# Expert weights laid out as 128 neighbouring rows per k tile, in a one-core encoder layer with a mixture of experts

## The chip, the cores and the metric

The kernel runs on one core of a Trainium2 chip. The metric is device time in microseconds, lower is better. A core has a matrix engine (PE, its weight loads are shown apart as PEld), a vector engine (DVE), a scalar engine (ACT), a general one (POOL), and a synchronising engine (SP) whose instruction stream issues here every DMA. The DMAs of the core are spread over 16 DMA engines.

## The reference

One layer of an encoder for 256 frames of width 2048, all float32. With everything but the last part in one line each:

```python
xn = rms_norm(h, norm_mix_g); proj = xn @ w_in + b_in             # attention and gating branches
merged = g_a * (y_a @ w_branch_a) + g_b * (y_b @ w_branch_b)
h = h + merged @ w_out
xn2 = rms_norm(h, norm_ffn_g)
# hierarchical mixture of experts: top-1 of 4 groups, top-2 of its 8 experts, 32 experts of width 256
hid = silu(t @ w_e_gate[e]) * (t @ w_e_up[e])                     # w_e_gate, w_e_up: (32, 2048, 256)
out = out + (hid * combine[:, e]) @ w_e_down[e]                   # w_e_down: (32, 256, 2048)
return rms_norm(h + out, norm_final_g)
```

The three expert weights are 201 MB of the 310 MB that the kernel moves.

## The kernel before

**Dense part.** All projections but the experts' run as "pieces" of a weight matrix. SP loads a piece of 1 MB (four k tiles of 128 rows by 512 columns) in two DMAs into one of four buffers `raw`; a weight row contributes 2 KB. ACT makes a rounded high part `whi` (line 529), DVE the rest `wlo` (line 831), and PE multiplies both with high and low parts of the activations (lines 1303 to 1305). The last four rounds are `w_out`; between them SP issues the first loads of expert weights.

**Router.** After the last dense round come the router and its top-k (from line 1511 on PE and line 1128 on DVE). A few matmuls whose result is not used (line 1310) fill PE's waits.

**Experts.** The 32 experts are taken in 8 quads of 4. An expert has room for 32 tokens, so a quad fills 128 columns. For each quad:

- `gather(qd)` (line 1602): for each of 16 k tiles PE multiplies the residual rows, as stationary operand, by the selection matrix `sel` of the quad. That picks the quad's tokens and turns them, two matmuls (two halves of the tokens) to a k tile. ACT (line 727) and DVE (line 1184) take the result out of PSUM into `xe`, times the gain of the norm for the 128 model columns of that k tile.
- `gate_up(qd, j, k4)` (line 1551): expert j against four k tiles of gate and up weights in one slot; the partial sums of four column groups are added by `fold_parts` (line 1568).
- `down`, `scatter`, and the addition into the residual (lines 1583, 1654, 1225).

`gather(qd + 1)` stands between the third and the fourth expert of quad qd; `gather(0)` stands alone, ahead of everything.

**Order of the loads.** The expert weights go through a ring of 18 slots of 1 MB. `load_slot(n)` fills one: a gate/up slot by two DMAs of 512 KB (line 435), a down slot by one DMA of 1 MB (line 428; line 431 for the last quad). A quad is 24 slots, 16 of gate and up and 8 of down; in all 192 slots. Slots 0 to 17 are loaded while the dense part runs, in pairs between the `w_out` rounds and then as dense buffers come free. From slot 18 on SP waits until PE has used slot n - 18, and issues in order.

**Which model rows a k tile holds.** With `"e (p k) f -> e p k f"` partition p holds rows 16p to 16p + 15, and k tile k is every sixteenth row. The four k tiles of a slot are then four neighbouring rows of 256 floats: one run of 4 KB in memory for each partition. The gather has to follow the same order, so it reads every sixteenth column of `resid`:

```python
rows = resid[:, t, :].rearrange("p (d k) -> p k d", k=KT)[:, 4 * q + h, :]
```

and the gain has to be loaded in that order too, as `gP` (line 417). The gains in the other order (column kt holds the gains of rows 128 kt to 128 kt + 127) lie already in `gT`, made at the kernel's start. The down weights are loaded in runs of 8 KB, for the last quad in runs of 2 KB.

A fallback (`If(more == 1)`) for experts with more than 32 tokens is not entered with these inputs.

Of the kernel before, what the change touches and what calls it, by code (L numbers as in the profile page):

```python
# [28 lines left out]
ALU = mybir.AluOpType  # L29
ACT = mybir.ActivationFunctionType  # L30
AX_X = mybir.AxisListType.X

P = 128
# [31 lines left out]
def build_trunk(nc, a, out):  # L65
    T, D = a["x"].shape[1], a["x"].shape[2]
    TT, KT = T // P, D // P
# [25 lines left out]
    with ExitStack() as ctx:  # L93
# [4 lines left out]
        def at(name, kb, shape, dt=F32):  # L98
            nbytes = 4
            for n in shape[1:]:  # L100
                nbytes *= n
            assert kb * KB + nbytes <= room, name
            return nc.alloc_sbuf_tensor_at(name, shape, dt, offset=base + int(kb * KB))

        def sem(name):
            return ctx.enter_context(nc.semaphore(name))
# [4 lines left out]
        resid = at("resid", 0, [P, TT, D])  # L111
# [56 lines left out]
        qT = at("qT", 197.5, [HEAD, T // CHUNK, Q_PER_KV, CHUNK])  # L168
        kT = at("kT", 201.5, [HEAD, T])
        prob = [at(f"prob{b}", 202.5 + 2 * b, [P, 4, P]) for b in range(2)]  # L170
        gP = at("gP", 199, [P, KT])
        wr = at("wr", 194.5, [P, KT, NR])
        small_at = [206.5]

# [11 lines left out]
        gT = small("gT", [P, 2 * KT])  # L186
# [61 lines left out]
        resid_in, g2_in, wr_in, br_in, gf_in = (sem(n) for n in ("resid_in", "g2_in", "wr_in", "br_in", "gf_in"))  # L248
# [35 lines left out]
        xe_full, xe_by_act, xe_by_dve = sem("xe_full"), sem("xe_by_act"), sem("xe_by_dve")  # L284
# [4 lines left out]
        f_in, f_xT_full, f_xT_made, f_gu_full = sem("f_in"), sem("f_xT_full"), sem("f_xT_made"), sem("f_gu_full")  # L289
# [60 lines left out]
        w_a_v, w_b_v = chunked(a["w_branch_a"]), chunked(a["w_branch_b"])  # L350
        b_in_v = a["b_in"].rearrange("a (c n) -> a c n", n=COLS)
        b_gate_v = a["b_gate"].rearrange("a (c n) -> a c n", n=COLS)
        wg_v = a["w_e_gate"][0].rearrange("e (p k) f -> e p k f", p=P)
        wu_v = a["w_e_up"][0].rearrange("e (p k) f -> e p k f", p=P)
        wd_v = a["w_e_down"][0].rearrange("e (k p) d -> e p k d", p=P)

        def wide(row):
# [5 lines left out]
        def _(sp):  # L363
# [50 lines left out]
            for t in range(TT):  # L414
                sp.dma_start(resid[:, t, :], x_v[:, t, :]).then_inc(resid_in, 16)
            sp.wait_ge(yaT_lo_made, NKV)
            sp.dma_start(gP[:], a["norm_ffn_g"].rearrange("a (p k) -> (a p) k", k=KT)).then_inc(g2_in, 16)
            sp.dma_start(wr[:, :, 0:NG], a["w_router_group"][0].rearrange("(k p) n -> p k n", p=P)).then_inc(wr_in, 16)
            sp.dma_start(wr[:, :, LG:NR], a["w_router_expert"][0].rearrange("(k p) n -> p k n", p=P)).then_inc(wr_in, 16)
            def load_slot(n):  # L420
# [70 lines left out]
            for u in range(2 * TT):  # L491
                t, h = divmod(u, 2)
# [30 lines left out]
        def _(act):  # L523
# [21 lines left out]
            for u in range(8):  # L545
# [3 lines left out]
                t, k4 = divmod(u, 4)  # L549
# [172 lines left out]
            def gathered_a(qd, q):  # L722

                act.wait_ge(xe_full, KT // 4 * qd + q + 1)
                for h in range(4):
                    kt = 4 * q + h
                    act.activation(xe[:, qd % 2, kt, :, :].rearrange("p e s -> p (e s)"),
                                   bank[6 + q % 2][:, h * P:(h + 1) * P], ACT.Copy,
                                   scale=gP[:, kt:kt + 1]).then_inc(xe_by_act, 1)

            def gate_up_out(qd, j):

# [57 lines left out]
            with act.If(more == 1):  # L790
                act.activation(table_junk[:, 0:1], ones[:, 0:1], ACT.Silu).then_inc(f_table, 1)
                act.wait_ge(f_table, 1)
                for t in range(TT):
                    for k4 in range(4):
                        act.wait_ge(f_xT_full, 4 * t + k4 + 1)
                        for k in range(4):
                            kt = 4 * k4 + k
                            act.activation(xT_f[:, kt, :], bank[6 + k4 % 2][:, k * P:(k + 1) * P],
                                           ACT.Copy, scale=gP[:, kt:kt + 1]).then_inc(f_xT_made, 1)
                    with act.Fori(0, NE) as e:  # L800
                        act.wait_ge(f_gu_full, e + (NE * t + 1))
                        act.activation(f_s[:], bank[0][:, 0:FF], ACT.Silu,
                                       scale=rstd[:, 2 * TT + t:2 * TT + t + 1]).then_inc(f_silu_made, 1)
                        act.wait_ge(f_hT_full, e + (NE * t + 1))
                        act.activation(f_hT[:], bank[1][:, 0:2 * P].rearrange("p (a b) -> p a b", a=2),
                                       ACT.Copy).then_inc(f_hT_made, 1)
                act.wait_ge(f_added, 4 * NE * TT + 4)
                act.wait_ge(sq_f_made, TT * NC)
                for b in range(NC):
                    final_squares(b, f_sq_made)  # L810
                act.wait_ge(f_hf, TT * NC)
                act.activation(table_junk[:, 0:1], ones[:, 0:1], ACT.Sqrt).then_inc(table_back, 1)
                act.wait_ge(table_back, 1)
            root(3)
            for t in range(TT):
                n = 3 * TT + t
                if t == 0:
# [3 lines left out]
                               scale=rstd[:, n:n + 1]).then_inc(y_by_act, 1)  # L821
# [3 lines left out]
        def _(dve):  # L825
# [75 lines left out]
            for h2 in range(2):  # L901
                rows = slice(h2 * CHUNK, (h2 + 1) * CHUNK)
# [199 lines left out]
            evac_out(0)  # L1102
            for k in range(1, ROUND):
                dense_lo(D_ROUND0 + 1, k)
            dve.wait_ge(g2_in, 16)
            with dve.Fori(2, NC) as n:
                dense_lo(n + D_ROUND0, 0)
                evac_out(n - 1)
# [73 lines left out]
            def gathered_v(qd, q):  # L1182
                dve.wait_ge(xe_full, KT // 4 * qd + q + 1)
                dve.tensor_tensor(xe[:, qd % 2, 4 * q:4 * q + 4, :, :].rearrange("p k e s -> p k (e s)"),  # L1184
                                  bank[6 + q % 2][:].rearrange("p (k n) -> p k n", k=4),
                                  gP[:, 4 * q:4 * q + 4].to_broadcast([P, 4, P]), ALU.mult).then_inc(xe_by_dve, 1)

            pick(0)
            gathered_v(0, 1)
# [69 lines left out]
            with dve.If(more == 1):  # L1259
# [9 lines left out]
                for t in range(TT):  # L1269
                    with dve.Fori(0, NE) as e:  # L1270
# [6 lines left out]
                        for b in range(NC):  # L1277
                            h = resid[:, t, b * COLS:(b + 1) * COLS]
# [22 lines left out]
        def _(pe):  # L1301
# [300 lines left out]
            def gather(qd):  # L1602

                pe.wait_ge(sel_made, qd + 1)
                for q in range(KT // 4):
                    if q == 0 and qd:
                        pe.wait_ge(selT_made, qd)
                        pe.wait_ge(added, 8 * (qd - 1))
                    if q == 2:
                        pe.wait_ge(xe_by_act, 8 * qd + 4)  # L1610
                    if q == 3:
                        pe.wait_ge(xe_by_dve, 2 * qd + 1)
                    for h in range(4):
                        for t in range(TT):
                            rows = resid[:, t, :].rearrange("p (d k) -> p k d", k=KT)[:, 4 * q + h, :]
                            mm = pe.matmul(bank[6 + q % 2][:, h * P:(h + 1) * P], rows,  # L1616
                                           sel[:, t, :, :].rearrange("p e s -> p (e s)"), start=t == 0, stop=t == TT - 1)
                    mm.then_inc(xe_full, 1)
# [77 lines left out]
            with pe.If(more == 1):  # L1696
                pe.wait_ge(added, 8 * NQ)
                for t in range(TT):
                    if t:
                        pe.wait_ge(f_added, 4 * NE * t + 4)  # L1700
                    for k4 in range(4):
                        if k4 > 1:
                            pe.wait_ge(f_xT_made, 16 * t + 4 * k4 - 4)
                        for k in range(4):
                            dst = bank[6 + k4 % 2][:, k * P:(k + 1) * P]
                            rows = resid[:, t, :].rearrange("p (d k) -> p k d", k=KT)[:, 4 * k4 + k, :]
                            mm = pe.matmul(dst, rows, ident[:], start=True, stop=True)
                        mm.then_inc(f_xT_full, 1)
                    pe.wait_ge(f_xT_made, 16 * t + 16)
                    with pe.Fori(0, NE) as e:  # L1710
                        pe.wait_ge(f_in, 48 * e + (48 * NE * t + 48))
                        pe.wait_ge(f_added, 4 * e + (4 * NE * t + 4))
                        for kt in range(KT):
                            mm = pe.matmul(bank[0][:], xT_f[:, kt, :], f_gu[:, :, kt, :], start=(kt == 0), stop=(kt == KT - 1))
                        mm.then_inc(f_gu_full, 1)
                        pe.wait_ge(f_hid_made, e + (NE * t + 1))
                        for f in range(2):
                            mm = pe.transpose(bank[1][:, f * P:(f + 1) * P], f_hid[:, f * P:(f + 1) * P], ident[:])
                        mm.then_inc(f_hT_full, 1)
                        pe.wait_ge(f_hT_made, e + (NE * t + 1))  # L1720
                        for f in range(2):
                            for b in range(NC):
                                mm = pe.matmul(bank[2 + b][:], f_hT[:, f, :], f_dn[:, f, b * COLS:(b + 1) * COLS],
                                               start=(f == 0), stop=(f == 1))
                        mm.then_inc(f_dn_full, 1)
# [22 lines left out]
```

## Time and profile before

| | |
|---|---|
| time, median of 3 runs | 1064.36 us (1061.12 to 1065.03) |
| the profiled execution: its own time | 1064.98 us |
| its span | 1063.3 us |
| PE busy | 977.3 us (92%) |
| PE weight loads busy | 687.6 us (65%) |
| DVE, ACT busy | 392.5 us (37%), 335.2 us (32%) |
| moved by DMA | 310.17 MB, mean 292 GB/s |
| mean granted PE clock | 0.971 |

The span runs from the first to the last instruction; the 1.7 us between it and the execution's time lie around it. "Busy" of PE counts overlapping matmuls as one stretch. The granted clock is given as a share of 2.4 GHz, so 0.50 is 1.2 GHz. Shares over the whole span mix the dense part (to about 578 us) with the experts (from there on).

### The profile page before, as it was taken

The numbers are of one execution on the slowest core, as the hardware profiler recorded it, in microseconds if no ns is written. First come the engines' busy times: TensorE is split into PE (matmuls) and PEld (weight loads), VectorE is DVE, ScalarE is ACT, GpSimd is POOL, SyncE is SP. The second block draws the span as 40 slices with busy tenths as digits, with TensorE's granted clock in tenths as the row PEclk, the third lists the DMA queues.
The fourth block names the chain that finished last, engine by engine and source line by source line (L and its number), as shares of the span: only waits on it lengthen the run. The fifth ranks groups of instructions, "written<-read, shape, count | busy, mean of one in ns | idle before, by whom it ended". The sixth has DMA issues, their size and how long they took to land.

```text
span 1063.3 us, 13009 instructions
## 1 busy us (share of the span) xinstructions
PE 977.3 (92%) x5154; PEld 687.6 (65%) x5154; DVE 392.5 (37%) x530; ACT 335.2 (32%) x485; POOL 2.7 (0%) x13
## 2 busy tenths in 40 slices
PE   6999999999999999999999899998888878788884
PEld 5888888788888888888888564554362625335221
DVE  5545556565455455565343102020202011020204
ACT  5335545654343333444443111111011111101123
POOL 1000000000000000000000000000000000000000
PEclk9999999999999999999999999999998999899968
DMA  9565444458666656767777599999999999999994
GB/s 318 198 207 171 165 162 158 163 172 263 222 198 198 203 191 216 246 210 255 256 261 277 215 393 415 413 411 416 409 418 409 416 412 412 416 409 418 409 396 172
DMA packets 108820, 310.17 MB, mean 292 GB/s; under 512 B 13241, under 2 KB 14305, under 8 KB 101345
## 3 DMA queue, kind: packets, MB, share of 16 engines
q1 hardware_dynamic: 108770, 309.46, 77.8%
q8 instruction: 36, 0.59, 0.2%
q14 instruction: 14, 0.11, 0.0%
HBM read 307.33 MB, written 2.10 MB: 291 GB/s over the span
## 4 chain that ended last, share of the span: by engine, by line
PE 68%; DMA 19%; SPq 7%; ACT 3%; DVE 2%; issue 1%; ACTq 0%; DVEq 0%
PE bank L1303 15%; PE bank L1305 15%; PE bank L1304 15%; DMA slot<-in_w_e_up 11%; DMA slot<-in_w_e_down 7%; PE bank L1564 6%; SPq L435 5%; PE bank L1616 4%; PE bank L1583 4%; PE bank L1654 2%; SPq L428 2%; PE bank L1572 1%; PE bank L1407 1%; PE bank L1431 1%; ACT whi L529 1%
## 5 line engine op out<-in xcount | busy, mean ns | idle before, releaser
L831 DVE TENSOR_TENSOR wlo<-raw,whi 128x2048 fp32r<-128x2048 f32 x92 | 210.7, 2291 | 211.3 <-ACT whi L529 211.3
L529 ACT ACTIVATE whi<-raw 128x2048 fp32r<-128x2048 f32 x92 | 176.2, 1916 | 257.6 <-PE bank L1305 257.6
L1303 PE MATMUL bank<-whi,actT_hi 128*128 128x512 f32 x608 | 240.0, 395 | 3.9 <-DVE actT_lo L862 2.2
L1305 PE MATMUL bank<-wlo,actT_hi 128*128 128x512 f32 x608 | 236.9, 390 | 0.0
L1304 PE MATMUL bank<-whi,actT_lo 128*128 128x512 f32 x608 | 236.8, 389 | 0.0
L1564 PE MATMUL bank<-slot,xe 128*32 128x512 f32 x1024 | 125.7, 618 | 24.2 <-DMA slot<-in_w_e_up 22.3
L1303 PEld LDWEIGHTS bank<-whi,actT_hi 128*128 128x128 f32 x608 | 114.2, 188 | 30.1 <-DVE wlo L831 2.8
L1305 PEld LDWEIGHTS bank<-wlo,actT_hi 128*128 128x128 f32 x608 | 114.2, 188 | 24.1
L1304 PEld LDWEIGHTS bank<-whi,actT_lo 128*128 128x128 f32 x608 | 114.2, 188 | 22.7
L1616 PEld LDWEIGHTS bank<-sel,resid 128*128 128x128 f32 x512 | 112.4, 311 | 6.9 <-issue 6.4
L1616 PE MATMUL bank<-sel,resid 128*128 128x128 f32 x512 | 113.9, 385 | 0.0
L1225 DVE TENSOR_TENSOR resid<-bank,resid 128x512 f32<-128x512 f32 x64 | 44.3, 691 | 149.7 <-PE bank L1654 149.6
L1583 PE MATMUL bank<-slot,hid 128*32 128x512 f32 x512 | 69.4, 690 | 26.0 <-DMA slot<-in_w_e_down 21.4
L1564 PEld LDWEIGHTS bank<-slot,xe 128*32 128x32 f32 x1024 | 30.0, 112 | 97.4 <-issue 73.7
L1654 PE MATMUL bank<-out_rows,selT 128*128 128x512 f32 x128 | 62.8, 613 | 3.5 <-ACT out_rows L746 1.7
L1583 PEld LDWEIGHTS bank<-slot,hid 128*32 128x32 f32 x512 | 18.1, 123 | 69.5 <-issue 64.0
L734 ACT ACTIVATE gu_rows<-bank 128x512 f32<-128x512 f32 x32 | 19.1, 597 | 139.1 <-PE bank L1564 139.1
L1184 DVE TENSOR_TENSOR xe<-bank,gP 128x512 f32<-128x512 f32 x16 | 11.1, 691 | 134.6 <-PE bank L1616 134.6
L1572 PEld LDWEIGHTS bank<-fold,gu_rows 128*128 128x128 f32 x256 | 32.5, 196 | 31.3 <-ACT gu_rows L734 26.5
L1654 PEld LDWEIGHTS bank<-out_rows,selT 128*128 128x128 f32 x128 | 20.0, 188 | 47.6 <-issue 47.6
L1217 DVE TENSOR_TENSOR hid<-bank,s_act 128x64 f32<-128x64 f32 x32 | 7.2, 225 | 107.9 <-ACT s_act L738 107.9
L746 ACT ACTIVATE out_rows<-bank 128x512 f32<-128x512 f32 x32 | 19.1, 597 | 83.0 <-PE bank L1583 83.0
(198 smaller groups left out, 670.2 us busy)
## 6 DMA issues: line engine op xcount, KB each, us to landing
slot<-in_w_e_gate SPq DMA_DIRECT2D x128, 512.0 KB, 14.6
slot<-in_w_e_up SPq DMA_DIRECT2D x128, 512.0 KB, 15.3
slot<-in_w_e_down SPq DMA_DIRECT2D x64, 1024.0 KB, 19.1
raw<-in_w_gate SPq DMA_DIRECT2D x64, 512.0 KB, 4.6
raw<-in_w_in SPq DMA_DIRECT2D x56, 512.0 KB, 4.8
raw<-in_w_out SPq DMA_DIRECT2D x32, 512.0 KB, 4.8
raw<-in_w_branch_a SPq DMA_DIRECT2D x16, 512.0 KB, 4.6
raw<-in_w_branch_b SPq DMA_DIRECT2D x16, 512.0 KB, 4.3
```

Source lines behind the costliest of these rows:

```text
L435: sp.dma_start(dst[:, h * KB:(h + 1) * KB].rearrange("p (k f) -> p k f", f=FF), w[QUAD * qd + j, :, 4 * k4:4 * k4 + 4, :]).then_inc(slot_i ...
L529: return act.activation(whi[slot][:], src, ACT.Copy)
L831: dve.tensor_tensor(wlo[s][:], raw[:, k, :], whi[s][:], ALU.subtract).then_inc(lo_made, 1)
L1225: dve.tensor_tensor(h, bank[dst][:], h, ALU.add).then_inc(added, 1)
L1303: pe.matmul(o, x_hi, w_hi, start=start, stop=False)
L1304: pe.matmul(o, x_lo, w_hi, start=False, stop=False)
L1305: return pe.matmul(o, x_hi, w_lo, start=False, stop=stop)
L1564: mm = pe.matmul(bank[j % 2][c * CAP:(c + 1) * CAP, :], xe[:, qd % 2, 4 * k4 + c, j, :], w[:, :, c, :], start=k4 == 0, stop=k4 == 3)
L1572: mm = pe.matmul(bank[j % 2][:, f * CAP:(f + 1) * CAP], gu_rows[j % 2][:, f * P:(f + 1) * P], fold[:], start=True, stop=True)
L1583: mm = pe.matmul(bank[2 + b][e * CAP:(e + 1) * CAP, :], hid[:, e, f * CAP:(f + 1) * CAP], w, start=f == 0, stop=f == 1)
L1616: mm = pe.matmul(bank[6 + q % 2][:, h * P:(h + 1) * P], rows, sel[:, t, :, :].rearrange("p e s -> p (e s)"), start=t == 0, stop=t == TT - 1)
L1654: pe.matmul(bank[dst][:], selT[:, t * P:(t + 1) * P], out_rows[:, b * COLS:(b + 1) * COLS], start=True, stop=True).then_inc(scat_full, 1)
```

## The change

The gate and up weights are read so that k tile k is the 128 neighbouring rows 128k to 128k + 127. A partition's part of a slot is then four runs of 1 KB, 128 rows apart in memory, where it was one run of 4 KB. The bytes, the slots, the tiles in SBUF and the matmuls are the same in number and size. The gather reads 128 neighbouring columns of `resid` in place of every sixteenth. The gain comes from the second half of `gT`, and `gP`, its DMA and DVE's wait for it are gone. The down weights are loaded as before.

```diff
-        gP = at("gP", 199, [P, KT])
...
-        wg_v = a["w_e_gate"][0].rearrange("e (p k) f -> e p k f", p=P)
-        wu_v = a["w_e_up"][0].rearrange("e (p k) f -> e p k f", p=P)
+        wg_v = a["w_e_gate"][0].rearrange("e (k p) f -> e p k f", p=P)
+        wu_v = a["w_e_up"][0].rearrange("e (k p) f -> e p k f", p=P)
...
-            sp.dma_start(gP[:], a["norm_ffn_g"].rearrange("a (p k) -> (a p) k", k=KT)).then_inc(g2_in, 16)
...
-                                   scale=gP[:, kt:kt + 1]).then_inc(xe_by_act, 1)
+                                   scale=gT[:, KT + kt:KT + kt + 1]).then_inc(xe_by_act, 1)
...
-            dve.wait_ge(g2_in, 16)
...
-                                  gP[:, 4 * q:4 * q + 4].to_broadcast([P, 4, P]), ALU.mult).then_inc(xe_by_dve, 1)
+                                  gT[:, KT + 4 * q:KT + 4 * q + 4].to_broadcast([P, 4, P]), ALU.mult).then_inc(xe_by_dve, 1)
...
-                            rows = resid[:, t, :].rearrange("p (d k) -> p k d", k=KT)[:, 4 * q + h, :]
+                            rows = resid[:, t, (4 * q + h) * P:(4 * q + h + 1) * P]
```

The fallback's reads of `resid` and of the gain change in the same way.

## Rows read from the trace of the kernel before

**Rows 1.** The page: DMA share and GB/s in 40 slices

```profile
span 1063.3 us, 13009 instructions
...
DMA  9565444458666656767777599999999999999994
GB/s 318 198 207 171 165 162 158 163 172 263 222 198 198 203 191 216 246 210 255 256 261 277 215 393 415 413 411 416 409 418 409 416 412 412 416 409 418 409 396 172
```

**Rows 2.** Windows (length, busy and count by engine, granted clock, DMA share, GB/s), whole stages

```profile
440.00:540.00 100.00, 100.00 (x483) 83.83 (x482) 52.72 (x41) 42.04 (x38) 0.00 (x0) 1.00 0.69 242
...
705.00:1015.00 310.00, 256.06 (x1571) 134.51 (x1571) 44.73 (x86) 42.07 (x107) 0.00 (x0) 0.95 1.02 413
```

**Rows 3.** Chain of waits in order of time (start, us, what), 578 us to the end

```profile
578.37 14.26 PE bank L1616 x64
592.72 0.69 DVE xe L1184
...
594.12 0.38 DVE fold L1207
594.54 5.38 PE bank L1564 x32
...
997.82 15.89 DMA slot<-in_w_e_up
1013.75 1.07 PE bank L1564 x8
1014.82 6.63 PE bank L1628 x8
```

**Rows 4.** Timeline of SP's DMA issues (start, us, line, tile, count)

```profile
248.08 0.54 SPq L418 DMA_DIRECT2D wr<-in_w_router_group  x1
248.67 7.50 SPq L419 DMA_DIRECT2D wr<-in_w_router_expert  x1
...
595.69 8.48 SPq L428 DMA_DIRECT2D slot<-in_w_e_down  x6
```

**Rows 5.** Windows: the idle queue before the experts, and the dip behind gather(1)

```profile
582.00:595.00 13.00, 11.07 (x54) 10.58 (x57) 3.52 (x14) 2.29 (x8) 0.00 (x0) 1.00 0.00 1
...
627.00:630.00 3.00, 2.42 (x24) 0.52 (x16) 0.00 (x0) 0.52 (x1) 0.00 (x0) 1.00 0.97 330
630.00:632.00 2.00, 1.30 (x12) 1.12 (x16) 0.50 (x2) 0.30 (x2) 0.00 (x0) 1.00 0.99 346
```

**Rows 6.** Windows: stretches with full queues, by length of the run in memory

```profile
20.50:22.50 2.00, 2.00 (x9) 1.66 (x10) 1.01 (x1) 2.00 (x2) 0.00 (x0) 1.00 1.10 286
...
714.00:734.00 20.00, 18.64 (x124) 13.08 (x123) 2.16 (x5) 2.43 (x8) 0.00 (x0) 1.00 1.02 422
745.00:775.00 30.00, 25.23 (x140) 12.34 (x141) 6.74 (x12) 3.77 (x10) 0.00 (x0) 1.00 1.03 409
...
1022.00:1040.00 18.00, 15.85 (x83) 5.20 (x82) 2.83 (x6) 3.22 (x7) 0.00 (x0) 0.71 1.05 387
```

**Rows 7.** DMA issues: tile, source, engine, count, KB each, median us to landing

```profile
slot<-in_w_e_gate SPq DMA_DIRECT2D x128, 512.0 KB, 14.6
...
slot<-in_w_e_down SPq DMA_DIRECT2D x64, 1024.0 KB, 19.1
...
wr<-in_w_router_expert SPq DMA_DIRECT2D x1, 256.0 KB, 10.3
```

**Rows 8.** Timeline of PE and its weight loads (start, us, engine, line, shapes, count)

```profile
218.22 3.77 PEld L1459 LDWEIGHTS bank<-proj,wspT 128*128 128x128 f32 x32
...
218.44 3.73 PE L1459 MATMUL bank<-proj,wspT 128*128 128x128 f32 x32
...
650.77 0.41 PE L1641 MATMUL bank<-ident,hot 128*128 128x128 f32 x2
...
660.05 14.24 PE L1616 MATMUL bank<-sel,resid 128*128 128x128 f32 x64
...
700.02 0.41 PE L1641 MATMUL bank<-ident,hot 128*128 128x128 f32 x2
```

**Rows 9.** Groups by line, shapes kept apart (busy us, mean ns, idle before)

```profile
L1616 PE MATMUL bank<-sel,resid 128*128 128x128 f32 x512 | 113.9, 385 | 0.0
...
L1616 PEld LDWEIGHTS bank<-sel,resid 128*128 128x128 f32 x512 | 112.4, 311 | 6.9 <-issue 6.4 <-DVE sel L1173 0.5
...
L1459 PEld LDWEIGHTS bank<-proj,wspT 128*128 128x128 f32 x32 | 3.7, 192 | 0.1
```

More of the change, by code:

```diff
@@ L798, in _ @@
                             act.activation(xT_f[:, kt, :], bank[6 + k4 % 2][:, k * P:(k + 1) * P],
-                                           ACT.Copy, scale=gP[:, kt:kt + 1]).then_inc(f_xT_made, 1)
+                                           ACT.Copy, scale=gT[:, KT + kt:KT + kt + 1]).then_inc(f_xT_made, 1)
                     with act.Fori(0, NE) as e:
@@ L1705, in _ @@
                             dst = bank[6 + k4 % 2][:, k * P:(k + 1) * P]
-                            rows = resid[:, t, :].rearrange("p (d k) -> p k d", k=KT)[:, 4 * k4 + k, :]
+                            rows = resid[:, t, (4 * k4 + k) * P:(4 * k4 + k + 1) * P]
                             mm = pe.matmul(dst, rows, ident[:], start=True, stop=True)
```

## The prediction

> **What bounds the kernel now.** I read the page's slices first, then windows, then the chain of waits. The slices [rows 1] split the span in two. Up to slice 22 (about 580 us) the DMA engines are 40 to 70% busy; from slice 23 on, for seventeen slices less the last, they are full and move 393 to 418 GB/s. The windows say the same of whole stages [rows 2]: in the dense part PE is busy 100.00 us of 100 and the DMA share is 0.69; from 705 to 1015 us PE is busy 256 us of 310 and the DMA share is 1.02. So PE sets the pace of the dense part and the stream of expert weights that of the experts. The chain of waits [rows 3] shows how they meet. From 578.37 us it is PE: gather(0), DVE's last extraction, `fold`, the first gate_up. Late in the experts it goes through loads of gate and up, up to the last slot of the third expert of the last quad, which lets PE go at 1013.75 us; from there it is PE and its followers, 49.6 us to the end of the span.
>
> The point that matters sits between the two. The 18 slots of the ring are full by 582 us and no load moves for 13 us [rows 5], because slot 18 needs PE to have used slot 0. PE does that right after gather(0), and SP's first new load goes out at 595.69 us [rows 4]. From there the queue stays full, so the time of the last weights is the restart plus the sum of all transfers, and PE's work inside the stage (its quad takes 700.02 - 650.77 = 49.25 us [rows 8]) is hidden under 24 slots of transfers, some 61 us.
>
> **The gather.** Its two operands are 128 by 128 floats; the weight load now steps over 16 floats per column. Such a load takes 311 ns where the same shape with neighbouring columns takes 192 [rows 9]. The spacing of the matmuls follows: 64 records in 14.24 us, 222 ns each, against 32 in 3.73 us, 117 ns each [rows 8], for the same shapes. New gather: 64 x 0.117 = 7.5 us, so 6.8 us less for each of 8. Bounds: nothing, and 14.24 / 2 = 7.1 us if the spacing falls to the moving operand's half. The spatial row is the same shape, so I take 6.8. The extraction keeps up: PE makes a bank in 1.9 us, ACT and DVE need about 1.1 and 0.7, and DVE's small operations behind it are off the path.
>
> Only gather(0) counts in full: it is alone on the chain and the queue is idle behind it, so the restart comes 6.8 us earlier. The other seven lie under full queues. One of them leaves a trace: while gather(1) runs PE frees no slot, and the queue thins to 330 GB/s for 3 us and 346 for 2 us [rows 5] against 409. That is 3 x (1 - 330/409) + 2 x (1 - 346/409) = 0.9 us lost, and with 6.8 us less it closes: SP has then twelve slots out, over 30 us of transfers, and waits only some 24 us. I take 1.0 us.
>
> **The loads.** What does a run of 1 KB cost? There is no such run in the trace, but runs of four other lengths with full queues [rows 6]. With 16 engines, the time that one takes for a run is 16 x length / rate:
>
> - 8 KB (down, issued just before 714 us): 16 x 8192 / 422 = 310.6 ns
> - 4 KB (gate and up): 16 x 4096 / 409 = 160.2 ns
> - 2 KB (down of the last quad): 16 x 2048 / 387 = 84.7 ns
> - 512 B (`wsp`, in the first 25 us): 16 x 512 / 286 = 28.6 ns
>
> They lie on a line: about 9.4 ns for each run and 36.7 ns for each KB. From 4 and 2 KB extrapolated, a 1 KB run takes 84.7 - 37.8 = 46.9 ns; between 2 KB and 512 B interpolated, 47.3. I take 47.0 ns, 349 GB/s. A load of 512 KB has 8 runs of 4 KB on each engine, 1.282 us, and will have 32 runs of 1 KB, 1.504 us: 0.222 us more. Bounds: half a 2 KB run (42.4 ns, 0.073 us more) and twice a 512 B run (57.2 ns, 0.548 us more).
>
> How many such loads count? 8 x 16 gate/up slots, less the 16 loaded before the restart, less the 4 behind the point where the chain leaves the loads: 108 slots, 216 loads. 216 x 0.222 = 48.0 us. The bounds give 15.8 and 118.
>
> The Trainium skill speaks of this twice. Its page "DMA: Bandwidth & Descriptors" (section "Specifications") gives 512 B as the smallest transfer at line rate; by that the loads would cost nothing and the sum would be -7.8 us. The rows disagree with it: 387 and 286 GB/s at 2 KB and 512 B against 409 at 4 KB. The same page of the Trainium skill (section "Why small descriptors are slow (HBM only)") counts about 3 cycles of overhead for a packet beside one for each 32 bytes; 1 KB would be 35 cycles, 4 KB 131, so 4 x 35 / 131 = 1.069. By that, an estimate, a load would cost 0.088 us more and the sum would be 0.088 x 216 - 7.8 = +11 us.
>
> **What is hidden.** The 32 gate/up loads before the restart take 7.1 us longer in all. Most fall where the DMA share is 0.69 and PE never waits; the 8 issued last, from 562 us on, delay the full ring by 1.8 us from 582 to 584, still ahead of the restart at 588.9; were all 7.1 us late it would be 589 us. The price without this cover would be those 7.1 us. The dense `raw` loads queued behind a pair of slots come 0.9 us later; they are four buffers ahead. The load of `gP` (8 KB, 0.6 us of SP) and DVE's wait were under PE's full stretch: nothing. ACT and DVE read a gain of the same shape.
>
> **SP and the queue.** Each load has 512 runs to be described where it had 128, in 1.504 us. The nearest row: the two router loads, 2048 runs each, were issued at 248.08 and 248.67 us, and the second landed 10.3 us after its issue, at 259.0 [rows 4, 7]. So 4096 runs were described, moved and landed in 10.9 us, at most 1.37 us for 512, though part of it was waiting behind other loads. It holds, with no great room. SP may be held longer by each issue, as it is now by a full queue; a load lands 14.6 us after its issue [rows 7], which is over eleven loads deep, so a shallower queue still feeds the engines.
>
> **The end.** From the point where the third expert's last slot lands, four slots of gate and up (8 x 0.222 = 1.8 us more) and 8 MB of down follow. In the old kernel PE trails there by several us, its clock at 0.50 after its waits, so I take the 49.6 us behind that point as they are, within 2 us.
>
> **The sum.** +48.0 (loads) - 6.8 (gather(0)) - 1.0 (dip) = +40.2 us. On the profiled execution's own time, 1064.98: 1105.2. It lies 0.6 us above the median of the runs, 1064.36, which I leave. I predict 1105 us, 3.8% slower.
>
> **Rivals.**
>
> 1. *Runs of 1 KB move as fast as 4 KB.* Then only the gather is left: 1064.98 - 7.8 = 1057 us, faster by 0.7%. The place is the 216 loads; it decides if a 1 KB run takes under 41 ns (0.036 us a load times 216 is 7.8 us). Nothing in the rows speaks for it, and the line through four lengths against it. 0.04. It is what the 512 B rule of the Trainium skill ("DMA: Bandwidth & Descriptors", section "Specifications") would have.
> 2. *A smaller cost for each run*, from the half 2 KB run or a little above, 42.4 to 45 ns: +8 to +26 us, 1073 to 1091 us. Nothing in the rows speaks for it but that the 512 B stretch is short (2 us) and other loads are in it. 0.09. The cycle count of the Trainium skill's same page would lie here, at 1076. A cost between this and rival 1, within 0.5% of no change, gets 0.03.
> 3. *Describing the runs becomes the bound.* Had the 7.50 us at which SP stood on the 2048-run load [rows 4] been all description, 512 runs would take 1.88 us, 0.59 more than now: +128 - 8 = +120, 1185 us. Against it: the landing at 259.0. It decides above 1.504 us for 512 runs. A mild form, a few per cent over, gives 1120 to 1140. 0.09.
> 4. *PE's clock.* With 68 us of transfers to 42.4 us of PE work in a quad (32 x 1.504 + 8 x 2.485 against 49.25 - 6.8), PE waits more, and waits are where its clock falls. The work would need most of its time at half clock to reach 68 us; above that point the experts are PE's again, up to 85 us a quad. Now the mean is 0.95 [rows 2]. 0.03, at 1110 to 1150.
>
> **Numbers.** The forecast has 0.72. A nanosecond on the 1 KB run is 32 x 216 = 6.9 us; from 45.3 to 49 ns and 2 us at the end the time runs from 1093 to 1119, and that holds 8 in 10 with the near parts of rivals 2 to 4; the other parts are left out. About 0.5% is what a measurement of this kernel can tell from no change: faster 0.04, within 0.5% 0.03, slower 0.93.
>
> **What the new profile would show.** PEld of line 1616 at 190 ns and gather at 7.5 us; SP's first down load after the pause near 589 us; windows inside the gate/up loads near 349 GB/s with a DMA share still above 1, and down windows still at 422; no dip behind gather(1); PE idle for about 25 us in 68. A DMA share clearly under 1 beside a low rate would be rival 3; 409 GB/s would be rival 1; a clock near 0.6 with PE busy would be rival 4.

## The result, and the profile after

The changed kernel takes 1105.21 us (median of 4 runs, 1104.25 to 1106.52); the kernel before, run beside it, 1063.11 us. The ratio is 1.0398 with a 95% interval of 1.038 to 1.0415, so 42 us slower. The profiled execution took 1104.35 us with a span of 1102.5 us, 39.2 us longer than that of before. The prediction was 1105 us.

The page of the changed kernel, its span and the same slices as in [rows 1], with the packets and the chain by line:

```profile
span 1102.5 us, 13008 instructions
...
DMA  9665445459666666759886999999999999999995
GB/s 313 195 208 181 154 141 173 160 171 293 208 197 206 202 202 200 247 179 321 260 281 283 349 369 380 348 401 348 373 377 349 401 349 377 373 348 400 347 364 223
DMA packets 206980, 310.16 MB, mean 281 GB/s; under 512 B 13097, under 2 KB 145233, under 8 KB 199505
...
PE 57%; SPq 27%; DMA 10%; ACT 2%; issue 2%; DVE 2%; ACTq 0%; DVEq 0%
SPq L433 25%; PE bank L1300 15%; PE bank L1302 15%; PE bank L1301 15%; DMA slot<-in_w_e_down 5%; DMA slot<-in_w_e_up 4%; PE bank L1561 3%; SPq L426 2%; PE bank L1613 2%; PE bank L1580 2%; PE bank L1404 1%; PE bank L1428 1%; ACT whi L527 1%; PE bank L1625 1%; PE bank L1307 1%
```

The slices of the dense part are much as before. In the experts those that hold only gate and up now read 347 to 349 GB/s, and mixed ones more. The engines are at least as full as before (the DMA share of such a stretch is 1.10, it was 1.02 to 1.03); they move less. The windows say it without the mixing: 620 to 650 us has gate and up in 1 KB runs, 660 to 670 us down in 8 KB runs (compare [rows 6]).

```profile
620.00:650.00 30.00, 29.24 (x205) 12.10 (x198) 6.73 (x12) 6.03 (x14) 0.00 (x0) 0.98 1.10 348
660.00:670.00 10.00, 4.26 (x29) 1.55 (x32) 0.56 (x2) 0.22 (x1) 0.00 (x0) 0.66 1.02 423
```

348 GB/s is 16 x 1024 / 348 = 47.1 ns for a run on one engine. The gather is as short as was costed, and the loads start again earlier (below, this is called the restart). The timeline of PE's weight loads and PE, and of SP (start, us), against [rows 3, 4]:

```profile
578.87 7.22 PEld L1613 LDWEIGHTS bank<-sel,resid 128*128 128x128 f32 x64 [0.45 <-DVE sel L1170]
578.88 7.41 PE L1613 MATMUL bank<-sel,resid 128*128 128x128 f32 x64
...
589.34 6.80 SPq L426 DMA_DIRECT2D slot<-in_w_e_down  x6
```

The chain of waits in order of time, its last part (against the last rows of [rows 3]):

```profile
1054.47 1.63 PE bank L1561 x8
...
1070.86 2.58 SPq L429
1073.49 14.32 DMA slot<-in_w_e_down
1087.85 1.07 PE bank L1580 x8
```

From these rows the 39.2 us can be split in three. The restart moved from 595.69 to 589.34 us, -6.35. From the restart to the landing of the last quad's third expert it was 1013.75 - 595.69 = 418.06 us and is 1054.47 - 589.34 = 465.13 us, +47.07. From there to the end of the span it was 49.55 us and is 48.03, -1.5. The sum is +39.2.

### The profile page after: what moved, and what is told of

It is laid out like the page before. It is cut to its first block, busy times and chain, and to the rows that moved or that the text cites. A ratio compares the mean times of both kernels' runs of the same rounds, so it can differ in the third digit from the quotient of the medians.

```text
span 1102.5 us, 13008 instructions
## 1 busy us (share of the span) xinstructions
PE 960.3 (87%) x5154; PEld 645.0 (59%) x5154; DVE 392.4 (36%) x530; ACT 335.3 (30%) x485; POOL 2.7 (0%) x13
## 4 chain that ended last, share of the span: by engine, by line
PE 57%; SPq 27%; DMA 10%; ACT 2%; issue 2%; DVE 2%; ACTq 0%; DVEq 0%
SPq L433 25%; PE bank L1300 15%; PE bank L1302 15%; PE bank L1301 15%; DMA slot<-in_w_e_down 5%; DMA slot<-in_w_e_up 4%; PE bank L1561 3%; SPq L426 2%; PE bank L1613 2%; PE bank L1580 2%; PE bank L1404 1%; PE bank L1428 1%; ACT whi L527 1%; PE bank L1625 1%; PE bank L1307 1%
## 5 line engine op out<-in xcount | busy, mean ns | idle before, releaser
L1561 PE MATMUL bank<-slot,xe 128*32 128x512 f32 x1024 | 133.6, 642 | 46.3 <-DMA slot<-in_w_e_up 44.3
L1580 PE MATMUL bank<-slot,hid 128*32 128x512 f32 x512 | 84.0, 812 | 63.0 <-DMA slot<-in_w_e_down 61.8
L1580 PEld LDWEIGHTS bank<-slot,hid 128*32 128x32 f32 x512 | 20.9, 144 | 119.0 <-issue 116.1
L1651 PE MATMUL bank<-out_rows,selT 128*128 128x512 f32 x128 | 68.6, 665 | 3.4 <-ACT out_rows L744 1.7
L1613 PEld LDWEIGHTS bank<-sel,resid 128*128 128x128 f32 x512 | 62.9, 206 | 8.8 <-issue 8.3
L1613 PE MATMUL bank<-sel,resid 128*128 128x128 f32 x512 | 64.4, 291 | 0.0
L1651 PEld LDWEIGHTS bank<-out_rows,selT 128*128 128x128 f32 x128 | 22.3, 206 | 52.3 <-issue 52.3
L1181 DVE TENSOR_TENSOR xe<-bank,gT 128x512 f32<-128x512 f32 x16 | 11.1, 691 | 100.4 <-PE bank L1613 100.4
```

Source lines behind the costliest of these rows:

```text
L1561: mm = pe.matmul(bank[j % 2][c * CAP:(c + 1) * CAP, :], xe[:, qd % 2, 4 * k4 + c, j, :], w[:, :, c, :], start=k4 == 0, stop=k4 == 3)
L1580: mm = pe.matmul(bank[2 + b][e * CAP:(e + 1) * CAP, :], hid[:, e, f * CAP:(f + 1) * CAP], w, start=f == 0, stop=f == 1)
L1651: pe.matmul(bank[dst][:], selT[:, t * P:(t + 1) * P], out_rows[:, b * COLS:(b + 1) * COLS], start=True, stop=True).then_inc(scat_full, 1)
```

## The experiments

Each is an edit of the kernel before and was timed beside it (medians 1062.35 to 1064.23 us). Line numbers are those of the kernel before, or a few more where lines were added; in the changed kernel they are two or three less. Where a cut shows only the deciding lines, `...` stands for the others.

**The loads alone.** Gate and up in 1 KB runs, with the gather of before. The rows of weights and of `xe` then don't match; the work is the same.

```diff
-        wg_v = a["w_e_gate"][0].rearrange("e (p k) f -> e p k f", p=P)
+        wg_v = a["w_e_gate"][0].rearrange("e (k p) f -> e p k f", p=P)
```

> The kernel before with the change's loads alone: gate and up in runs of 1 KB, the gather still in steps of 16 columns. The order of the weight rows no longer matches that of the gathered rows, so the experts' result is another, with the same work. My theory: each run costs a DMA engine about 9.4 ns beside its bytes, 0.222 us for each of 216 loads on the path, so 1064.4 + 48 = 1112 us, and the restart of the loads stays at 595.7 us, the gather at 14.2 us. Rival, that part of the +42 comes from elsewhere (an earlier end of the gather that leaves PE cooler, later loads in the dense part): then this run is within a few us of 1105 or well above 1115.

1110.93 us against 1062.78, ratio 1.0459 (1.0438 to 1.048): +48.1 us. SP's first load after the pause is at 595.78 us. The third expert's last slot landed at 1061.07 us, 47.3 us later than in the kernel before with the same restart; that is 0.219 us for each of 216 loads, where 0.222 was predicted. That point in the chain of waits of this kernel:

```profile
1061.07 1.94 PE bank L1564 x8
```

**The gather alone.** The gather of the change, with loads and `gP` of before; here too only the order does not match.

```diff
-                            rows = resid[:, t, :].rearrange("p (d k) -> p k d", k=KT)[:, 4 * q + h, :]
+                            rows = resid[:, t, (4 * q + h) * P:(4 * q + h + 1) * P]
```

> The kernel before with the change's gather alone: neighbouring columns of resid, weights still in runs of 4 KB (their row order then does not match, the work is the same). My theory: gather(0) 6.8 us shorter is worth 6.8 us through the earlier restart, and the closed dip 1.0 us: 1057 us, restart at 589 us, no stretch under 400 GB/s behind gather(1). Rival: all eight gathers count (8 x 6.8 = 54 us): 1010 us. Rival: none counts, because the stream or PE catches up: 1064 us.

1055.25 us, ratio 0.9925 (0.9911 to 0.9939): -7.5 us. The restart is at 589.46 us, and no window of 3 us from 618 to 639 us reads under 407 GB/s. All eight gathers became about 6.8 us shorter, 54 us of PE's work in all, and 7.5 came out at the end. With the loads alone the two parts add to +40.6 us; the change measured +42.1, which the intervals (about 2 us each) don't tell apart.

**Cut in SBUF, not in memory.** The memory side stays a run of 4 KB for each partition, and it lands as four runs of 1 KB with gaps. All else is the kernel before.

```diff
-                        sp.dma_start(dst[:, h * KB:(h + 1) * KB].rearrange("p (k f) -> p k f", f=FF),
+                        sp.dma_start(dst[:].rearrange("p (k u f) -> p u k f", u=2, f=FF)[:, h, :, :],
...
-                w = slot[n % RING][:].rearrange("p (u k f) -> p u k f", u=2, k=4)
+                w = slot[n % RING][:].rearrange("p (k u f) -> p u k f", u=2, k=4)
```

> The kernel before with the k tiles of gate and up interleaved in the slot: a partition's part of a load is still one run of 4 KB in memory, but lands in SBUF as four runs of 1 KB, 2 KB apart. Weight order, gather and result are those of before. My theory (a cost for each run, whichever side cuts it, paid by the DMA engine): like 1 KB runs in memory, 349 GB/s, +48 us: 1112 us. Rival (memory: the cost comes from reading rows 128 KB apart): 1064 us, 409 GB/s.

1112.92 us, ratio 1.0473 (1.0451 to 1.0495): +50.1 us, as with the cut in memory. The window of 700 to 715 us of this kernel:

```profile
700.00:715.00 15.00, 13.34 (x78) 4.88 (x76) 5.77 (x11) 1.43 (x4) 0.00 (x0) 1.00 1.10 349
```

The same 349 GB/s. The count of packets says why:

```profile
DMA packets 207125, 310.17 MB, mean 279 GB/s; under 512 B 13242, under 2 KB 145378, under 8 KB 199650
```

It is 207125 with the loads alone too, and 108820 in the kernel before: about 384 more for each of 256 loads, as 512 runs in place of 128 give. So it is not the 128 rows between two runs that cost. A run is what is contiguous on both sides, and each one has its price.

**Half of that length.** The same idea with gate and up interleaved by 128 columns: 512 B runs in SBUF.

```diff
-                        sp.dma_start(dst[:, h * KB:(h + 1) * KB].rearrange("p (k f) -> p k f", f=FF),
-                                     w[QUAD * qd + j, :, 4 * k4:4 * k4 + 4, :]).then_inc(slot_in[n % RING], 16)
+                        sp.dma_start(dst[:].rearrange("p (k u f) -> p u k f", u=2, f=P)[:, h, :, :],
+                                     w[QUAD * qd + j, :, 4 * k4:4 * k4 + 4, :].rearrange("p k (g f) -> p (k g) f", f=P)).then_inc(slot_in[n % RING], 16)
...
```

> As the kernel with gate and up landing in runs of 1 KB in SBUF, now in runs of 512 B (gate and up interleaved by halves of a k tile); 4 KB runs in memory; the matmuls read their 512 weight columns in four stretches. The result is the reference's. The line through the run lengths gives 28.3 ns a run, 64 runs for each engine and load, 1.81 us where 4 KB has 1.28: +0.53 x 216 = +115 us, 1178 us, with a DMA share above 1. Rival, describing the runs is already the bound at 1.46 us for 512 runs (the spacing of SP's issues with runs of 1 KB): 1024 runs take 2.92 us, +1.64 x 216 = +354 us, 1417 us, with a DMA share near 0.6.

1187.03 us, ratio 1.1173 (1.1155 to 1.119): +124.7 us, where the line through the run lengths gave +115. A window inside the loads (1125 to 1141 us), and one of SP's issues in it:

```profile
1125.00:1141.00 16.00, 12.45 (x32) 3.03 (x32) 0.00 (x0) 2.39 (x4) 0.00 (x0) 0.50 1.19 290
```

```profile
1132.34 1.74 SPq L435 DMA_DIRECT2D slot<-in_w_e_up  x1
```

Two readings. First, 290 GB/s is 28.2 ns for 512 B, on the line. The last four slots, too, are now on the path, since PE no longer trails there: 224 loads x (64 x 0.0282 - 1.282) = 117 us, an estimate that leaves 8 us. Second, SP issues a load of 1024 runs every 1.78 us here. In the changed kernel it issued one of 512 runs every 1.46 us, which looked like a price for describing runs. Were it so, 1024 would take 2.92 us. So describing is not the bound at 1 KB: there SP is held by the full queue.

At 512 B SP isn't clear of the bound everywhere. Not all stretches look like the one above: 935 to 940 us reads 266 GB/s at a DMA share of 0.96, 1090 to 1095 us 265 at 0.98, and 1110 to 1115 us 240 at 0.87, though SP stands in issues back to back, of 1.47 and 1.49 us just after 1092 us. The DMA engines are less full there, so at least a part of the 8 us lies in such stretches. That describing limits them is likely but not shown.

**Runs of 2 KB, gather in steps of 2.** The k tiles in pairs: partition p holds rows 256a + 2p and 256a + 2p + 1.

```diff
-        wg_v = a["w_e_gate"][0].rearrange("e (p k) f -> e p k f", p=P)
+        wg_v = a["w_e_gate"][0].rearrange("e (a p b) f -> e p a b f", p=P, b=2)
...
-                            rows = resid[:, t, :].rearrange("p (d k) -> p k d", k=KT)[:, 4 * q + h, :]
+                            rows = resid[:, t, :].rearrange("p (a d b) -> p a b d", d=P, b=2)[:, (4 * q + h) // 2, (4 * q + h) % 2, :]
```

> Gate and up in runs of 2 KB (two neighbouring rows to a partition, k tiles in pairs), the gather steps over 2 columns (8 bytes). The result is the reference's. The loads by the line through the run lengths: 84.7 ns a run, 16 runs, 1.355 us a load, 0.073 x 216 = +16 us. The gather: if a weight load is fast only with neighbouring columns, 15 us as with a step of 4: 1062.8 + 16 = 1079 us; if a step of 2 still has two columns in each 16 bytes and is halfway, 11 us: 1076; if it is as fast as neighbouring columns, 1071.

1071.79 us, ratio 1.0097 (1.0077 to 1.0118): +9.4 us, near the third of the three cases (1071 us). The slices with gate and up alone read 386 to 387 GB/s, and SP's restart is at 589.12 us. The gather's weight loads (ns, least, median, most; first and last start):

```profile
L1616 PEld LDWEIGHTS bank<-sel,resid x512: 193/196/333, 578.2 to 967.7; 128*128 128x128 f32 x171
```

**Runs of 4 KB, gather in steps of 4.** The same with `b=4`: slot k4 holds rows 512 k4 + 4p + b, 4 KB in one run again.

> Slot k4 of gate and up holds model rows 512 k4 + 4p + b, b = 0 to 3: runs of 4 KB in memory as before, while the gather steps over 4 columns (16 bytes) in place of 16 (64 bytes). The result is the reference's. If the price of a stepped weight load comes with the distance in bytes, a step of 4 may be as cheap as neighbouring columns: gather 7.5 us, total 1057 us, faster than both. Rival: any step costs (each column its own access): gather 14.2 us and 1064 us. In between: a step of 4 at 240 ns and 1060 us.

1064.26 us, ratio 1.0021 (1.0008 to 1.0033): nothing gained, rather 1.5 us lost. The same row of this kernel:

```profile
L1616 PEld LDWEIGHTS bank<-sel,resid x512: 307/329/332, 578.4 to 969.4; 128*128 128x128 f32 x171
```

gather(0) takes 15.2 us here, 1.0 us more than with the step of 16, and the restart is at 597.30 us, 1.6 us later than before. So 4 KB runs and a cheap gather don't go together in this way.

**The change for quad 0 alone.** Its 16 gate/up slots are loaded before the restart. Only they come in 1 KB runs, and only gather(0) reads neighbouring columns and takes its gain from `gT`.

```diff
-                    for h, w in enumerate((wg_v, wu_v)):
+                    for h, w in enumerate((wg_v, wu_v) if qd else (wg0_v, wu0_v)):
...
-                            rows = resid[:, t, :].rearrange("p (d k) -> p k d", k=KT)[:, 4 * q + h, :]
+                            rows = (resid[:, t, :].rearrange("p (d k) -> p k d", k=KT)[:, 4 * q + h, :] if qd
+                                    else resid[:, t, (4 * q + h) * P:(4 * q + h + 1) * P])
```

> The change for quad 0 alone: its 16 gate/up slots, which all land before the restart, in runs of 1 KB, and gather(0) over neighbouring columns; quads 1 to 7 as before, 4 KB runs and the stepped gather. The result is the reference's. My theory: the seven other gathers and the 32 slower loads are hidden, the restart comes at 589 us, and nothing slows the stream: 1062.8 - 6.8 = 1056 us (the dip behind gather(1) stays, so 0.5 to 1 us above the run with the gather alone, 1055.3). Rival: the slower loads before the restart fill the ring late or delay the dense loads: 1059 to 1063 us.

1055.28 us, ratio 0.9931 (0.9919 to 0.9943): -7.1 us. This is the whole gain of the gather with none of the loads' loss. It shows three steps of the prediction at once: the seven other gathers are hidden, so are the 32 slower loads ahead of the restart, and gather(0) works through the restart, here at 588.90 us.

```profile
578.44 7.41 PE L1619 MATMUL bank<-sel,resid 128*128 128x128 f32 x64
...
588.90 2.90 SPq L430 DMA_DIRECT2D slot<-in_w_e_down  x4
```

**Runs of 8 KB.** The line through the run lengths also says what the other direction is worth. A slot holds eight k tiles of gate or of up, loaded by one DMA of 1 MB, and PE reads from two slots at once. The slots therefore lie in pairs in SBUF, PE waits for both of a pair, and SP until both have been used.

```diff
-                    for h, w in enumerate((wg_v, wu_v)):
-                        sp.dma_start(dst[:, h * KB:(h + 1) * KB].rearrange("p (k f) -> p k f", f=FF),
-                                     w[QUAD * qd + j, :, 4 * k4:4 * k4 + 4, :]).then_inc(slot_in[n % RING], 16)
+                    w, k8 = (wg_v, wu_v)[k4 % 2], 8 * (k4 // 2)
+                    sp.dma_start(dst[:].rearrange("p (k f) -> p k f", f=FF),
+                                 w[QUAD * qd + j, :, k8:k8 + 8, :]).then_inc(slot_in[n % RING], 16)
...
+                w = pair[n0 % RING // 2][:, :, :].rearrange("p u (k f) -> p u k f", k=8)[:, :, 4 * (k4 % 2):4 * (k4 % 2) + 4, :]
```

> Runs the other way: a slot holds eight k tiles of gate or of up (one DMA of 1 MB, 8 KB runs), two slots together serve eight k tiles; the gather as before. The result is the reference's. The line gives 8 runs of 310.6 ns, 2.485 us for 1 MB where 4 KB has 2.564: -0.079 for each of 108 slots, -8.5 us. Against it, PE waits for two slots at a time and frees two at a time; at the end of the stream it has eight k tiles to do behind the last landing in place of four, 1 to 1.7 us. Together 1062.8 - 7.5 = 1055 us. Rival, the cost for a run is the same for all lengths above 4 KB: 1063 to 1065 us.

1055.4 us, ratio 0.993 (0.9918 to 0.9943): -7.0 us. The stretch that read 409 GB/s in [rows 6] reads 420:

```profile
745.00:775.00 30.00, 26.71 (x141) 13.35 (x142) 6.74 (x12) 3.77 (x10) 0.00 (x0) 0.94 1.01 420
```

The 7.0 us are not the price of the runs alone. SP's restart:

```profile
598.75 7.51 SPq L430 DMA_DIRECT2D pair<-in_w_e_down  x6
```

That is 3.1 us later than in the kernel before. From the restart to the last bytes of weights (by windows of 1 us, about 1039 us here and 1045.5 us before) it takes about 440 us where it took 450, close to the 8.5 us that the line gave.

**Both gains.** Quad 0 in the order of the change, the other quads in 8 KB runs.

> Both gains together: quad 0 in the change's order (now in 1 KB runs of 1 MB loads, before the restart) with gather(0) over neighbouring columns, quads 1 to 7 in 8 KB runs with the stepped gather. The result is the reference's. My theory: the two are separate, one earlier restart (-7.0 us measured) and one faster stream (-7.0 us measured): 1062.5 - 14 = 1048.5 us. Rival: they share a cause (both only close the pause at the restart or the same slack at the end): 1052 to 1055 us.

1048.43 us against 1064.23, ratio 0.9849 (0.9833 to 0.9865): -15.8 us. It is faster than the kernel before and than the changed one. The two gains taken singly give 14.1 us; with an interval of 1.7 us on the 15.8 they add, within what the runs can tell. The restart is at 590.88 us, 4.8 us earlier than in the kernel before, and the stream from there again takes about 440 us.

## Why the prediction was right

**What bounds.** PE in the dense part, the stream of weights in the experts, joined by the restart behind gather(0): shown by the gather alone (54 us less work on PE, 7.5 us less time) and by the change for quad 0 alone.

**The gather.** For gather(0), predicted 7.5 us and 192 ns a weight load; measured 7.41 us, and a median of 192 ns over all eight gathers. The restart was predicted at 588.9 us and came at 589.34; `sel` was 0.5 us later in that execution. The slower loads of the dense part are not the reason, by the kernel with the loads alone, where gather(0) starts at 578.48 us, 0.1 us later than before.

**What is hidden.** The ring was full by 583 us, 1 us later than before and over 6 us ahead of the restart; 584 was predicted. Quad 0 alone shows the same in the time.

**The loads.** This is the term that carries the result. 47.0 ns for a 1 KB run came from four other lengths in the old trace; 47.1 was measured. +48.0 us was the sum; the loads alone gave +48.1. The prediction writes the line with a slip: 36.7 ns for each KB would give 46.1 ns for 1 KB and 156 ns for 4 KB, which its own four lengths contradict. With 9.4 ns a run they want 37.6 ns a KB. The forecast did not use the wrong figure; the 47.0 ns came from the neighbouring lengths. With 37.6 the line held at 2 KB (386 to 387 GB/s) and in the full stretches at 512 B (290 GB/s) as well. That the price is one for each run, whichever side cuts it, was not in the prediction; the cut in SBUF showed it. What within the DMA engine takes the time stays open. Two rules on the page "DMA: Bandwidth & Descriptors" of the Trainium skill were rivals. The 512 B of "Specifications" would have made the loads free; the runs disagree, with 348 GB/s at 1 KB and 386 at 2 KB against 409 at 4 KB. The cycles of "Why small descriptors are slow (HBM only)" would have given, by an estimate, +19 us for the loads where 48 were measured; the sign is right, the size too small by more than half.

**The dip.** Predicted 1.0 us, from rows that gave 0.9. It isn't there in the changed kernel (346 to 350 GB/s in every window of 3 us from 618 to 639 us), but its worth can't be told from the timings: with the dip's cause removed (the gather alone) 1055.25 us, with gather(1) as before (quad 0 alone) 1055.28. In the latter the dip is shallow, 401 and 382 GB/s in two windows of 3 us.

**SP.** It did not bind, as predicted. But the chain of waits now gives SP's issues 25% of the span, and a reader could take that for the bound. At 1 KB an issue takes the time that a full queue makes it wait: the rate beside it is 348 GB/s at a DMA share of 1.10, and with 512 B runs SP issues twice as many runs in 1.78 us as here in 1.46. Landing came down from 14.6 to 8.1 us after issue for `gate`, and no dry queue is seen behind the restart. The room is small, though: the thin stretches of the kernel with 512 B runs have the sign that the prediction named for rival 3, a DMA share under 1 beside a low rate.

**The end.** I took the part behind the third expert as it was, within 2 us; it got 1.5 us shorter. The reason given, that PE trails there, no longer holds: now PE waits for the last down weights (14.32 us in the chain), so less is left after they land. That outweighed the 1.8 us that the four slots of gate and up were costed at.

**The clock.** The mean granted clock fell from 0.971 to 0.924, and 660 to 670 us, where PE waits for down weights, has 0.66. No effect on the end is seen: behind the landing at 1054.47 us the last gate and up weights flow at 349 to 354 GB/s, and from 1064 us the down weights at 381 to 387 GB/s without a gap up to 1084 us, with PE's clock at 0.50 until 1068. Rival 4 had the direction right and no effect.

**What was luck.** The steps are right, but that 1105 us and 1105.21 agree so closely is luck in part. The sum was put on the profiled execution, 1064.98 us, while the median of the kernel before beside the changed one was 1063.11. Against medians the change cost 42.1 us, not 40.2, and between the two profiled executions 39.4. The terms, too, were off by 0.5 us at the restart and 1.5 at the end, in opposite directions.

## What to carry to other kernels

Before changing a layout for the sake of an on-chip operand, count the contiguous runs that the transfers will have on both sides, and fit their price from the lengths that the trace already holds; here two numbers, 9.4 ns a run and 37.6 ns a KB, gave the rate of every stretch with a full queue within 1%, from 512 B to 8 KB. A faster operation is worth little while the transfer queue is full, and all of its gain where the queue is idle and waits for it (54 us less work on PE gave 7.5 us here): find that one place and change only there. One layout need not serve all stages: the loads that are hidden can pay for the gather that is not.

## What the runs showed of the hardware that was not expected

The price of a stepped weight load of 128 by 128 floats isn't in proportion to the step. The medians are 192 ns for neighbouring columns, 196 for a step of 8 bytes, 329 for 16 bytes, and 312 for 64 bytes. A step of two floats is nearly free, a step of four costs the most, slightly more than sixteen. The time of gather(0) follows: 7.41, 7.80, 15.20 and 14.24 us. Why four costs more than sixteen is open.
